# Two more value units in the first eight retention steps, and the first merge set begun four steps later

## The chip, the cores and the metric

One core of a Trainium2 chip runs the whole kernel. The metric is the device time of one execution in microseconds (us); below is better. TensorE (PE in the profile) does the matmuls, its weight loads are listed apart as PEld; VectorE is DVE, ScalarE is ACT, GpSimd is POOL, and SyncE (SP) only issues DMAs and waits for semaphores.

## The reference

One decoder layer on 1,024 tokens of width 1,024, in float32. An input projection of the normed `x` gives ten parts. Two branches are computed from them and merged:

```python
y_mla = mla_branch(...) * silu(gate_mla)            # 8 heads of causal softmax attention, 1024 wide
y_ret = retention_branch(q, k, v, ...) * silu(gate_ret)   # 4 heads, chunks of 128 tokens, v is 2048 wide
merged = sigmoid(merge_mla) * (y_mla @ w_proj_mla) + sigmoid(merge_ret) * (y_ret @ w_proj_ret)
x = x + gate * (merged @ w_out)
```

Retention runs chunk by chunk with a state of 256 x 512 per head: the output of a chunk is `((q k^T) * decay) v + q R`, then `R` is decayed and `k^T v` added, and the output is normalised over 512 values. The value projection `h @ w_in[:, v_ret]` (1024 x 1024 by 1024 x 2048) is a plain matrix product, and so is `y_mla @ w_proj_mla`.

## The kernel before, in words

Every float32 operand is split in two halves (hi on ACT, lo on DVE, each as a rounded type that PE reads), and a product is three matmuls: hi by hi, hi by lo, lo by hi. Every engine's program is one list in a fixed order, written out by hand; an engine waits where it stands.

**The two stages that matter.** Attention is 64 steps (8 heads x 8 query blocks, `STEPS`), named g here with i = g mod 8. In step g PE does the scores of block g (`scores`, L2199 to L2203), half of the step's filler, the values of an earlier pair of blocks in odd steps (L2218 to L2220), the transposes of the probabilities of block g-1 (L2240) and the other half of the filler. `scores(g)` waits until the exponential of block g-1 has been read out of the same PSUM banks (`exp_done`). DVE masks the scores (L1691) and finds their maximum (L1693), ACT takes the exponential (L1283) and then reads its sum out (a second ACT instruction on L1283), DVE normalises. Retention is 32 steps (4 heads x 8 chunks, `CHUNK_STEPS`), named n, with m = n mod 8. In step n PE does the outputs of the chunk (L2289 to L2297; only three matmuls of 512 columns when m = 0), the state (L2307 to L2309; not when m = 7), filler, the key transposes and inner scores of the next chunk, filler, the transposes of the normalised output (`turn_outputs`, L2320) and a last share of filler. DVE's list in step n: the merges of finished set units, statistics of the output (L1794 and on), the low halves of the state (L1810), the masking and halves of the next inner scores (L1770 to L1778), the gated output (L1818), the low halves of the queries and keys two chunks ahead (L1330), and then whatever splits are planned for that step. `turn_outputs` needs ACT's normalised output `out_n` (L1362), and the next outputs need DVE's `inner_lo` (L1778).

**The filler** is matmul work without dependence on the step around it, cut in products of one matmul of 512 columns:

- The *value fill* (`fill`, L2132): 32 units (`FILL_UNITS`), each 24 products (`UNIT`): the value projection for one head and one block of 128 tokens. It is summed in bank `FILL_BANKS[unit % 3]`, evicted by ACT (`evict_fill`, L1319) and DVE (`lower_fill`, L1670) into `v_stage`, and stored by a DMA of GpSimd (`store_fill`, L1055). A unit may begin when the unit three before it, whose bank it takes, is lowered. How many products are done by the end of attention step g stands in `fill_plan`: 42 before the first step, then `FILL_STEP[i]` in every step, `FILL_END` in the three steps behind the last, and `FILL_LATE[n]` in the first retention steps.
- The *first merge set* (`fill_set`, L2164): 16 units of 24 products, `y_mla @ w_proj_mla`, by `set_plan`. Its inputs are loaded and split in the retention steps that `MERGE_LOAD`, `MERGE_SPLIT`, `SET0_LOAD` and `SET0_SPLIT` name.

**Weights of the value fill.** Each group of 8 units (one head of values) has its weights in four parts. Products 12p to 12p+12 of the last pair of units of a group free part p (`parts_used`). In the next step's list SP loads the part of the next group (`load_weight`, L504), ACT splits it behind the copies of the transposed probabilities (`split_weight`, L524, 1,024 columns) and DVE lowers it (`lower_weight`, L530). All these loads but two go through one raw place, so a load waits until the part before it has been lowered. If the last-but-one unit of a group was finished in the step before, its eviction stands ahead of the exponential (`filled_ahead`).

**GpSimd** rotates the queries and keys of chunk n (`rotate_chunk`, L1046 to L1051) as soon as the outputs of chunk n-3 are done. The last two value units are stored ahead of the rotation of chunk 9. The rotated chunk n is rounded by ACT in retention step n-2 (`high_qk`, L1326).

Of the kernel before, what the change touches and what calls it, by code (L numbers as in the profile page):

```python
# [18 lines left out]
ACT = mybir.ActivationFunctionType  # L19
# [5 lines left out]
KD = D // P  # L25
# [60 lines left out]
FILL_UNITS = V_GROUPS * NT  # L86
R_MERGE = len(SEQ)
SETS = 3
MERGE_LOAD = (1, 4, 5, 7)
MERGE_SPLIT = (2, 5, 7, 10)  # L90
SET0_LOAD = {2: (2, 3), 3: (4, 5), 4: (6, 7)}
SET0_SPLIT = {0: (0,), 1: (1,), 3: (2,), 4: (3, 4), 5: (5,), 6: (6, 7)}
# [6 lines left out]
FILL_BANKS = (2, 1, 3)  # L99
# [14 lines left out]
FILL_STEP = [12, 12, 11, 11, 10, 9, 9, 7]  # L114
FILL_END = [12, 10, 8]
FILL_LATE = [12, 12, 12, 12]
UNIT = 3 * KD
CHUNK_STEPS = H_RET * NT


class Layer:
# [267 lines left out]
    def counts(self):  # L389
# [8 lines left out]
        for n in range(CHUNK_STEPS):  # L398
            first, between, last = 12 * max(n - 3, 0), n - 7, 16 * (n - CHUNK_STEPS + 4)
            if last > 0:  # L400
                self.set_plan.append((2 * KD - 2) * UNIT + last)
            elif between > 0:
                self.set_plan.append(2 * UNIT + (2 * KD - 4) * UNIT * between // (CHUNK_STEPS - 11))
            else:
                self.set_plan.append(first)
# [198 lines left out]
    def parts_used(self, step):  # L604

        return sum(2 * UNIT * (4 * g + 3) + 12 * (part + 1) <= self.filled_by(step)
                   for g in range(V_GROUPS - 1) for part in range(V_PARTS))

# [247 lines left out]
    def sync_retention(self, sp):  # L856
        d = self.d
        units = 0
        for n in range(CHUNK_STEPS):
# [6 lines left out]
            if n == 6:  # L866
                self.load_t(sp, 0)
                self.load_t(sp, 1)
# [96 lines left out]
    def gpsimd(self, pool):  # L965
# [59 lines left out]
        for n in range(2, CHUNK_STEPS):  # L1025
            if n == 9:
                for unit in range(units, FILL_UNITS):
                    self.store_fill(pool, unit)
            self.rotate_chunk(pool, n)
# [278 lines left out]
    def evict_fill(self, act, unit):  # L1308
        act.wait_ge(self.fill_summed, unit + 1)
        if unit == 0:  # L1310
            act.wait_ge(self.raw_stored, 16 * RAW)
        elif unit == 1:
            for slot in range(3):
                act.wait_ge(self.split_stored[slot], self.store_count[slot])
        elif unit == 3:
            act.wait_ge(self.v_up_stored[2], 16 * 4)
        if self.v_stores(unit):
            act.wait_ge(self.v_stored[self.v_slot(unit)], 16 * self.v_stores(unit))
        self.nc.scalar.activation(self.v_place(unit)[:, 0, :], self.p[:, FILL_BANKS[unit % 3], :], ACT.Copy,  # L1319
                                  scale=self.t["ret_cols"][:, unit:unit + 1]).then_inc(self.v_hi_ready, 1)  # L1320
# [23 lines left out]
    def scalar_retention(self, act):  # L1344
        nc, p, t = self.nc, self.p, self.t
        units = 0
        for n in range(CHUNK_STEPS):
# [20 lines left out]
            if n == len(FILL_LATE) - 1:  # L1368
                for unit in range(FILL_UNITS - 2, FILL_UNITS):
                    self.evict_fill(act, unit)  # L1370
# [296 lines left out]
    def lower_fill(self, dve, unit):  # L1667
        dve.wait_ge(self.v_hi_ready, unit + 1)
        stage = self.v_place(unit)
        self.nc.vector.scalar_tensor_tensor(out=stage[:, 1, :], in0=self.p[:, FILL_BANKS[unit % 3], :],  # L1670
# [110 lines left out]
    def vector_retention(self, dve):  # L1781
        nc, p, t = self.nc, self.p, self.t
        units = 0
        for n in range(CHUNK_STEPS):
# [37 lines left out]
            if n == len(FILL_LATE) - 1:  # L1822
                for unit in range(FILL_UNITS - 2, FILL_UNITS):
                    self.lower_fill(dve, unit)
# [290 lines left out]
    def fill(self, pe, upto):  # L2115

        while self.filled < upto:
# [6 lines left out]
            if k == 0 and kind == 0:  # L2124
                if unit < 3:
                    pe.wait_ge(self.evicted, self.raws + RAW - 1)
                else:
                    pe.wait_ge(self.v_lo_ready, unit - 2)
# [3 lines left out]
            ins = self.nc.tensor.matmul(self.p[:, FILL_BANKS[unit % 3], :], h[:, k, tok], w[:, cut],  # L2132
# [133 lines left out]
    def inner_scores(self, pe, n):  # L2266
# [3 lines left out]
        if n == 1:  # L2270
            pe.wait_ge(self.v_lo_ready, FILL_UNITS - 2)
# [297 lines left out]
```

## Time and profile before

| | |
|---|---|
| median of 3 runs | 1616.3 us |
| lowest, highest | 1615.83, 1621.77 us |
| profiled execution, span from first to last instruction | 1616.2 us |
| attention, first scores to first retention outputs | 759.9 to 1101.4 us |
| retention, 32 steps | 1101.4 us to about 1347 us |

The only time that the profiled execution left is its span; no other time of its own is recorded, and the span stands 0.1 us under the median of the runs. Of the profile, PE's busy share says little here, since a busy PE can be one whose matmuls are stretched by waits inside the pipeline. What counts is the start of one matmul against the start of the next, the idle time in square brackets behind a row and the engine named there, and the granted clock (PEclk, 1.00 is full speed).

### The profile page before, as it was taken

How to read it: one execution, taken by the hardware profiler on the slowest of the kernel's cores; microseconds unless marked ns; L12 is line 12 of the kernel's file. 1: busy time of each engine (PE TensorE's matmuls, PEld its weight loads, DVE VectorE, ACT ScalarE, POOL GpSimd, SP SyncE). 2: the span in 40 equal slices, each digit the busy share in tenths (PEclk: the TensorE clock that was granted, in tenths of full speed). 3: DMA queues.
4: the chain of work that ended last, by engine and by line, in shares of the span. 5: the costliest groups of instructions: out<-in, count | busy, mean ns of one | idle time of the engine just before them, and what ended most of it. 6: DMA issues, size and time to landing. Idle time of an engine off the chain costs nothing. (4 is left out here: it accounts for less than half of the span.)

```text
span 1616.2 us, 20288 instructions
## 1 busy us (share of the span) xinstructions
PE 1568.4 (97%) x7568; PEld 1308.9 (81%) x7568; DVE 959.4 (59%) x1626; ACT 605.1 (37%) x1057; POOL 322.0 (20%) x280
## 2 busy tenths in 40 slices
PE   5999999999999999999999999899999999999998
PEld 4778888888888888798888888787688888888886
DVE  6984444444444457752566665567987775647544
ACT  5444333333333343342343433334544443213111
POOL 2232223322322200200000000015655530000000
PEclk9999999999999999999999999999999999999999
DMA  9132332223323334799265554447977767345422
GB/s 385 38 130 105 111 112 110 107 109 115 120 104 111 95 97 164 301 414 322 82 209 170 181 184 164 179 137 260 323 235 228 250 204 281 115 137 183 143 105 78
DMA packets 142225, 278.70 MB, mean 172 GB/s; under 512 B 11056, under 2 KB 83632, under 8 KB 133552
## 3 DMA queue, kind: packets, MB, share of 16 engines
q1 hardware_dynamic: 125488, 245.09, 43.6%
q10 hardware_dynamic: 12032, 15.54, 2.9%
q0 software_dynamic: 4608, 16.78, 2.7%
q8 instruction: 61, 1.00, 0.2%
q14 instruction: 36, 0.29, 0.1%
HBM read 182.47 MB, written 94.37 MB: 171 GB/s over the span
## 5 line engine op out<-in xcount | busy, mean ns | idle before, releaser
L1579 DVE TENSOR_TENSOR w_form<-w_pair,w_form 128x512 fp32r<-128x512 f32 x150 | 116.3, 776 | 127.2 <-ACT w_form L1211 125.6
L1211 ACT ACTIVATE w_form<-w_pair 128x512 fp32r<-128x512 f32 x150 | 94.6, 632 | 245.3 <-PE p_banks L2093 237.2
L2090 PE MATMUL p_banks<-h_hi,w_form 128*128 128x512 f32 x300 | 116.8, 389 | 1.1 <-DVE w_form L1579 1.1
L2093 PE MATMUL p_banks<-h_hi,w_form 128*128 128x512 f32 x300 | 116.7, 389 | 0.0
L2092 PE MATMUL p_banks<-h_lo,w_form 128*128 128x512 f32 x300 | 116.7, 389 | 0.0
L1283 ACT ACTIVATE prob<-p_banks,neg_max 128x128 f32<-128x128 f32 (+3 forms) x64 | 47.5, 742 | 182.9 <-DVE neg_max L1693 182.9
L524 ACT ACTIVATE w_hi<-w_raw 128x1024 fp32r<-128x1024 f32 (+2 forms) x69 | 59.5, 866 | 144.9 <-PE p_banks L2348 96.2
L2348 PE MATMUL p_banks<-y_hi,w_lo 128*128 128x512 f32 x256 | 99.6, 389 | 0.0
L2347 PE MATMUL p_banks<-y_lo,w_hi 128*128 128x512 f32 x256 | 99.6, 389 | 0.0
L2346 PE MATMUL p_banks<-y_hi,w_hi 128*128 128x512 f32 x256 | 99.6, 389 | 0.0
L1055 POOL DMA_DIRECT2D v_ret<-v_stage x32 | 17.7, 554 | 410.1 <-DVE v_stage L1670 410.0
L530 DVE TENSOR_TENSOR w_lo<-w_raw,w_hi 128x1024 fp32r<-128x1024 f32 (+3 forms) x70 | 72.0, 1033 | 35.4 <-ACT w_hi L524 34.7
L2132 PE MATMUL p_banks<-w_hi,h_hi 128*128 128x512 f32 x192 | 78.8, 410 | 0.6 <-DVE w_lo L530 0.6
L1008 POOL TENSOR_TENSOR w_pair<-w_pair 128x512 f32<-128x512 f32 x25 | 32.5, 1299 | 232.2 <-DVE w_form L1579 232.2
L2090 PE MATMUL p_banks<-h_sum_hi,w_form 128*128 128x512 f32 x200 | 77.9, 389 | 0.0
L2093 PE MATMUL p_banks<-h_sum_hi,w_form 128*128 128x512 f32 x200 | 77.8, 389 | 0.0
L2092 PE MATMUL p_banks<-h_sum_lo,w_form 128*128 128x512 f32 x200 | 77.8, 389 | 0.0
L2090 PE MATMUL p_banks<-h_forms,w_form 128*128 128x512 f32 x200 | 77.8, 389 | 0.0
L2092 PE MATMUL p_banks<-h_forms,w_form 128*128 128x512 f32 x200 | 77.8, 389 | 0.0
L2093 PE MATMUL p_banks<-h_forms,w_form 128*128 128x512 f32 x200 | 77.8, 389 | 0.0
L2132 PE MATMUL p_banks<-w_lo,h_hi 128*128 128x512 f32 x192 | 76.6, 399 | 0.0
L2132 PE MATMUL p_banks<-w_hi,h_lo 128*128 128x512 f32 x192 | 76.5, 398 | 0.0
(316 smaller groups left out, 4302.7 us busy)
## 6 DMA issues: line engine op xcount, KB each, us to landing
w_pair<-in_w_pairs SPq DMA_DIRECT2D x25, 1024.0 KB, 4.9
w_raw<-in_w_dense SPq DMA_DIRECT2D x45, 512.0 KB, 4.7
v_ret<-v_stage POOLq DMA_DIRECT2D x32, 512.0 KB, 3.4
v_chunk<-v_ret SPq DMA_DIRECT2D x32, 512.0 KB, 3.7
merge_t<-act_t SPq DMA_DIRECT2D x48, 256.0 KB, 3.4
act_t<-stage SPq DMA_DIRECT2D x40, 256.0 KB, 2.0
act_t<-stage_late SPq DMA_DIRECT2D x40, 256.0 KB, 2.0
ada<-in_w_ada SPq DMA_DIRECT2D x4, 2048.0 KB, 23.9
```

What stands on the lines that cost most here:

```text
L524: self.nc.scalar.activation(self.hi_place(r), self.raw_place(r), ACT.Copy).then_inc(self.w_hi_ready, 1)
L530: self.nc.vector.tensor_tensor(self.lo_place(r), self.raw_place(r), self.hi_place(r).bitcast(F32), ALU.subtract)\
L1211: self.nc.scalar.activation(self.form[f % FORM_SLOTS][:, 0, :], self.form_source(f), ACT.Copy).then_inc(self.form_hi, 1)
L1283: nc.scalar.activation(self.prob[:, g % 2, 0:width], p[:, 6:8, :].rearrange("p a n -> p (a n)")[:, 0:width], ACT.Exp, bias=self.neg_max[:, ...
L1579: nc.vector.tensor_tensor(self.form[f % FORM_SLOTS][:, 1, :], self.form_source(f), self.form[f % FORM_SLOTS][:, 0, :].bitcast(F32), ALU.su ...
L2090: self.nc.tensor.matmul(out, w_hi[:, cut], x_hi[:, q, :], start=fresh and q == 0, stop=False, skip_group_check=True)
L2092: self.nc.tensor.matmul(out, w_hi[:, cut], x_lo[:, q, :], start=False, stop=False, skip_group_check=True)
L2093: last = self.nc.tensor.matmul(out, w_lo[:, cut], x_hi[:, q, :], start=False, stop=q == KD // 2 - 1, skip_group_check=True)
L2132: ins = self.nc.tensor.matmul(self.p[:, FILL_BANKS[unit % 3], :], h[:, k, tok], w[:, cut], start=(k == 0 and kind == 0), stop=(k == KD - 1 ...
L2346: self.nc.tensor.matmul(out, self.w_hi[:, slot, cut], self.y_hi[y][:, tok], start=(k == 0), stop=False)
L2347: self.nc.tensor.matmul(out, self.w_hi[:, slot, cut], self.y_lo[y][:, tok], start=False, stop=False)
L2348: return self.nc.tensor.matmul(out, self.w_lo[:, slot, cut], self.y_hi[y][:, tok], start=False, stop=(k == KD - 1))
```

## The change

The steps of attention lose 6 filler products per head (`FILL_STEP` from a sum of 81 to one of 75), 48 in all, and `FILL_LATE` holds 12 products for eight retention steps in place of four. So 28 of the 32 units are done at the first retention step, not 30. Units 28 to 31 take banks 1 and 2 by turns, since bank 3 holds the inner scores. They are evicted in retention steps 1, 3 and 7 and stored ahead of the rotations of chunks 4, 6 and 11. Loads and splits of the first merge set move to later steps, the set begins in step 8, and its 288 middle products are spread over 17 steps and not 21.

```diff
-MERGE_LOAD = (1, 4, 5, 7)
-MERGE_SPLIT = (2, 5, 7, 10)
-SET0_LOAD = {2: (2, 3), 3: (4, 5), 4: (6, 7)}
-SET0_SPLIT = {0: (0,), 1: (1,), 3: (2,), 4: (3, 4), 5: (5,), 6: (6, 7)}
+MERGE_LOAD = (5, 8, 9, 11)
+MERGE_SPLIT = (6, 9, 11, 14)
+SET0_LOAD = {6: (2, 3), 7: (4, 5), 8: (6, 7)}
+SET0_SPLIT = {0: (0,), 2: (1,), 7: (2,), 8: (3, 4), 9: (5,), 10: (6, 7)}
...
-FILL_STEP = [12, 12, 11, 11, 10, 9, 9, 7]
+FILL_STEP = [11, 11, 10, 10, 9, 9, 8, 7]
 FILL_END = [12, 10, 8]
-FILL_LATE = [12, 12, 12, 12]
+FILL_LATE = [12] * 8
+LATE_UNIT = {1: (28,), 3: (29,), 7: (30, 31)}
+LATE_STORE = {4: (28,), 6: (29,), 11: (30, 31)}
+LATE_UNITS = 4
...
-            first, between, last = 12 * max(n - 3, 0), n - 7, 16 * (n - CHUNK_STEPS + 4)
+            first, between, last = 12 * max(n - 7, 0), n - 11, 16 * (n - CHUNK_STEPS + 4)
...
-                self.set_plan.append(2 * UNIT + (2 * KD - 4) * UNIT * between // (CHUNK_STEPS - 11))
+                self.set_plan.append(2 * UNIT + (2 * KD - 4) * UNIT * between // (CHUNK_STEPS - 15))
...
+    def fill_bank(self, unit):
+
+        return FILL_BANKS[unit % 3] if unit < FILL_UNITS - LATE_UNITS else 1 + unit % 2
...
-            if n == 6:
+            if n == 10:
                 self.load_t(sp, 0)
                 self.load_t(sp, 1)
...
-            if n == 9:
-                for unit in range(units, FILL_UNITS):
-                    self.store_fill(pool, unit)
+            for unit in LATE_STORE.get(n, ()):
+                self.store_fill(pool, unit)
             self.rotate_chunk(pool, n)
...
-            if n == len(FILL_LATE) - 1:
-                for unit in range(FILL_UNITS - 2, FILL_UNITS):
-                    self.evict_fill(act, unit)
+            for unit in LATE_UNIT.get(n, ()):
+                self.evict_fill(act, unit)
...
-            if n == len(FILL_LATE) - 1:
-                for unit in range(FILL_UNITS - 2, FILL_UNITS):
-                    self.lower_fill(dve, unit)
+            for unit in LATE_UNIT.get(n, ()):
+                self.lower_fill(dve, unit)
...
-                    pe.wait_ge(self.v_lo_ready, unit - 2)
+                    pe.wait_ge(self.v_lo_ready, unit - (2 if unit <= FILL_UNITS - LATE_UNITS else 1))
...
-            pe.wait_ge(self.v_lo_ready, FILL_UNITS - 2)
+            pe.wait_ge(self.v_lo_ready, FILL_UNITS - LATE_UNITS)
```

## Rows read from the trace of the kernel before

**Rows 1.** The page's head: the span, and PE's busy time, share and instructions.

```profile
span 1616.2 us, 20288 instructions
PE 1568.4 (97%) x7568; PEld 1308.9 (81%) x7568; DVE 959.4 (59%) x1626; ACT 605.1 (37%) x1057; POOL 322.0 (20%) x280
```

**Rows 2.** Busy time by stretch: the stretch, its length, each engine (instructions), PEclk, DMA, GB/s.

```profile
200.00:300.00 100.00, 100.00 (x443) 82.79 (x442) 45.65 (x65) 36.69 (x64) 27.62 (x20) 1.00 0.30 111
759.90:1101.40 341.50, 333.79 (x1902) 288.98 (x1901) 209.62 (x448) 123.02 (x269) 24.87 (x37) 0.99 0.50 168
1133.50:1173.80 40.30, 36.59 (x177) 27.53 (x176) 36.54 (x86) 23.25 (x44) 23.19 (x24) 1.00 0.98 324
```

**Rows 3.** Who waited for whom, PE: us in total, times, the longest.

```profile
PE p_banks L2199 <- ACT prob L1283: 7.5, 3, 3.5
PE p_banks L2320 <- ACT out_n L1362: 5.6, 9, 1.1
```

**Rows 4.** Instructions in order of time, PE at the end of step 35 (start, duration, idle before).

```profile
935.80 0.39 PE L2132 MATMUL p_banks<-w_hi,h_hi 128*128 128x512 f32 x1
938.43 0.50 PE L2199 MATMUL p_banks<-k_even,q_even 128*128 128x512 f32 x1 [2.24 <-ACT prob L1283]
```

**Rows 5.** In order of time: end of the sum's read-out, next scores (ends of steps i = 4, 6).

```profile
899.60 0.20 ACT L1283 ACTIVATION_READ_ACCUMULATOR prob<-p_banks,neg_max 128x1 f32 x1
900.01 0.40 PE L2199 MATMUL p_banks<-k_odd,q_odd 128*128 128x512 f32 x1
...
870.08 0.19 ACT L1283 ACTIVATION_READ_ACCUMULATOR prob<-p_banks,neg_max 128x1 f32 x1
870.32 0.50 PE L2199 MATMUL p_banks<-k_even,q_even 128*128 128x512 f32 x1
```

**Rows 6.** In order of time: two weight parts in adjacent steps, and the scores behind them.

```profile
1009.84 1.05 ACT L524 ACTIVATE w_hi_aside<-w_raw 128x1024 fp32r<-128x1024 f32 x1
1012.18 0.33 SPq L504 DMA_DIRECT2D w_raw<-in_w_dense  x1
1016.92 1.06 ACT L524 ACTIVATE w_hi<-w_raw 128x1024 fp32r<-128x1024 f32 x1 [2.98 <-DMA w_raw<-in_w_dense]
1020.79 0.19 ACT L1283 ACTIVATION_READ_ACCUMULATOR prob<-p_banks,neg_max 128x1 f32 x1
1021.03 0.50 PE L2199 MATMUL p_banks<-k_even,q_even 128*128 128x512 f32 x1 [1.75 <-ACT prob L1283]
```

**Rows 7.** Landing of the weight loads in attention; one slow load; PEclk behind it.

```profile
DMA to landing us min/median/max: 3.6/3.8/12.0
...
1027.92 0.35 SPq L504 DMA_DIRECT2D w_raw<-in_w_dense  x1
...
1035.26 1.06 ACT L524 ACTIVATE w_hi<-w_raw 128x1024 fp32r<-128x1024 f32 x1 [3.87 <-DMA w_raw<-in_w_dense]
...
1040.00:1050.00 10.00, 9.90 (x44) 8.47 (x45) 4.87 (x10) 3.00 (x7) 0.00 (x0) 0.69 0.04 13
```

**Rows 8.** In order of time, retention step 4: splits at its head, statistics, the transposes, next outputs.

```profile
1135.31 1.40 DVE L1670 SCALAR_TENSOR_TENSOR v_stage<-p_banks,ret_cols,v_stage 128x512 fp32r<-128x512 f32 x2
...
1137.76 0.69 DVE L1794 BATCH_NORM_STATS2 stats<-p_banks 128x6 f32<-128x512 f32 x1
...
1140.78 0.66 PE L2320 MATMUL p_banks<-ident,out_n 128*128 128x128 f32 x4 [1.07 <-ACT out_n L1362]
...
1142.41 0.50 PE L2289 MATMUL p_banks<-v_chunk,inner_hi 128*128 128x512 f32 x1
```

**Rows 9.** In order of time, DVE: the same split beside a rotation on GpSimd, and without.

```profile
1110.39 2.31 DVE L1839 TENSOR_TENSOR y_lo<-y_raw,y_hi 128x1024 fp32r<-128x1024 f32 x1
...
1118.72 1.21 DVE L1839 TENSOR_TENSOR y_lo<-y_raw,y_hi 128x1024 fp32r<-128x1024 f32 x1
```

**Rows 10.** In order of time: the rotation of chunk 4 begins; ACT rounds the rotated chunk.

```profile
1114.12 1.28 POOL L1046 TENSOR_TENSOR qk_by_sine_early<-qk_raw 128x512 f32<-128x512 f32 x1
...
1125.63 0.62 ACT L1326 ACTIVATE qk_chunk<-qk_raw 128x512 fp32r<-128x512 f32 x1
```

More of the change, by code:

```diff
@@ L1318, in evict_fill @@
             act.wait_ge(self.v_stored[self.v_slot(unit)], 16 * self.v_stores(unit))
-        self.nc.scalar.activation(self.v_place(unit)[:, 0, :], self.p[:, FILL_BANKS[unit % 3], :], ACT.Copy,
+        self.nc.scalar.activation(self.v_place(unit)[:, 0, :], self.p[:, self.fill_bank(unit), :], ACT.Copy,
                                   scale=self.t["ret_cols"][:, unit:unit + 1]).then_inc(self.v_hi_ready, 1)
@@ L1669, in lower_fill @@
         stage = self.v_place(unit)
-        self.nc.vector.scalar_tensor_tensor(out=stage[:, 1, :], in0=self.p[:, FILL_BANKS[unit % 3], :],
+        self.nc.vector.scalar_tensor_tensor(out=stage[:, 1, :], in0=self.p[:, self.fill_bank(unit), :],
                                             scalar=self.t["ret_cols"][:, unit:unit + 1], in1=stage[:, 0, :].bitcast(F32),
@@ L2131, in fill @@
             w = self.lo_place(r) if kind == 2 else self.hi_place(r)
-            ins = self.nc.tensor.matmul(self.p[:, FILL_BANKS[unit % 3], :], h[:, k, tok], w[:, cut],
+            ins = self.nc.tensor.matmul(self.p[:, self.fill_bank(unit), :], h[:, k, tok], w[:, cut],
                                         start=(k == 0 and kind == 0), stop=(k == KD - 1 and kind == 2))
```

## The prediction

> **What bounds the kernel now.** I read the page's head first: PE is busy for 97% of the span [rows 1], so what can be won is PE's own stalls. The list of who waited for whom names the two places where this change acts: scores that wait for an exponential, 7.5 us in 3 waits, and the output transposes of retention that wait for the normalised output, 5.6 us in 9 [rows 3]. The view by stretch adds what these lists hide: retention steps 4 to 8 have a PE busy 36.59 of 40.30 us beside a DVE busy 36.54 [rows 2]; that stretch is bound by DVE, the rest of retention by PE.
>
> A filler product costs what a matmul of 512 columns costs at full speed, 100 us / 443 = 0.226 us [rows 2]. The same work stays on PE wherever the plan puts it. **So the 48 moved products are worth nothing by themselves**: attention loses 48 x 0.226 = 10.8 us, retention gains 10.8. Only stalls decide, in four places.
>
> **1. Steps in which attention already waits.** The shortest time from the read-out of an exponential's sum to the next scores is 0.05 us: 1020.79 + 0.19 to 1021.03, a real wait [rows 6]. At the end of an i = 6 step it is 870.08 + 0.19 to 870.32, also 0.05 [rows 5]. There PE arrives no later than the exponential, so the product taken from that step (9 to 8) leaves a hole: 8 heads x 0.23 = **+1.8**. At the end of i = 4 the slack is 900.01 - 899.80 = 0.21, 0.16 above the least [rows 5]; a product less leaves 0.06, **+0.5** over 8 heads. The other steps that lose one had about 1 us or more. Bounds: 0 if those steps' other waits move along, +3.6 if every product taken from i = 4 and 6 is lost whole.
>
> **2. The weight parts.** Before, parts are freed in steps 10, 11, 13, 14; 29, 31, 32, 33; 48, 49, 51, 52 (the fill plan crossing 156, 168, 180, 192 and so on, 192 products to a group). Rows 6 show what two adjacent steps cost. A split at 1009.84 must be lowered before the next load goes out at 1012.18, the load's data come 4.7 us later, and ACT, which has the next exponential behind that split, sits idle for 2.98 us; PE then idles 1.75. The three such waits are the 7.5 us of [rows 3]: 2.24 [rows 4], 1.75 [rows 6] and 3.5, the last behind a load that took 7.3 us, 1027.92 to 1035.26 [rows 7], because query and key loads had gone out in front of it. After that wait PEclk is 0.69 over 10 us [rows 7]: 6.2 us at 1.2 instead of 2.4 GHz, 3.1 us lost. Together **10.6 us**.
>
> By the new plan parts are freed in 11, 12, 14, 15; **32, 33, 34, 35**; 52, 53, 55, 56. From one split to the next at least 2.3 (ACT and DVE) + 3.6 to 4.7 (landing, [rows 6, 7]) = 5.9 to 7.0 us pass, while an attention step lasts 341.5 us / 67 = 5.1 [rows 2], and steps 34 to 36 about 4. The middle group needs three intervals in a row: 18 to 21 us against some 13.5 of steps; with the slacks there (1, 1.4 us) I get 2.6 us idle ahead of scores(36). A second effect: the last two units of a group now end in the same step (6 and 7 in 15, 14 and 15 in 35, 22 and 23 in 56), so the unit after next asks for a bank that DVE has only just got to. DVE lowers unit 14 behind the part, the mask, the maximum and the gated output, some 2.5 us after the part; PE stands at its third product after the transposes. That makes 3.4 us in step 36, and by the same working 1.8 in step 16 and 2.0 in step 57. The first group adds 1.0 in step 14, where the slack is nil. Sum 1.0 + 1.8 + 2.6 + 3.4 + 2.0 = 10.8, so **+0.2**. The third group's long wait goes, the second's takes its place. Bounds: 4 (landings of 3.6, units lowered in time) and 18 (a landing of 7.3, and the half clock behind the second group).
>
> **3. The DVE-bound steps of retention.** In step 4, DVE's backlog (two unit lowerings, 1.40, and a 1.21 split) puts the statistics off to 1137.76; the transposes follow 3.02 later with 1.07 idle, and the next outputs 4.65 after the statistics [rows 8]. After the change steps 4 to 6 carry none of these splits, and their stalls (about 1.6 + 0.8 + 0.8) go. But the same splits stand in steps 7 to 11, and step 8 is the first of a head: six output matmuls fewer, 1.4 us, hide less. It stays 8.9 us long, 3.0 of them stall; steps 9 to 11 give 0.8 each, step 12 (two merges and a weight) 0.5, step 7 0.3. Before, this stretch is 3.7 us idle by [rows 2], and 6.4 by the starts of its matmuls in steps 4 to 12 (stretched matmuls hide the rest); after, 0.3 + 3.0 + 2.4 + 0.5 = 6.2: **-0.2**. Bounds: 3 and 9.
>
> **4. Denser filler behind.** From step 12 on 17 products a step stand in place of 14, two of the three ahead of the transposes, 0.45 us. Steps 15 and 23, where no state is computed, waited 0.67 and 0.19 idle, some 0.8 and 0.3 in the starts; 1.0 of that goes. Stalls of steps 0 to 3 are the same, but the stored unit 28 now goes ahead of the rotation of chunk 4 on GpSimd. That rotation began at 1114.12 and is used at 1125.63 [rows 10]; behind the lowering of unit 28 (about 1119.5) and a store of 0.55 it ends near 1124.2, still in time. But the next one then runs beside DVE's split. A split took 2.31 us beside a rotation and 1.21 alone [rows 9]; of that 1.1 I take 0.3, with 0 and 1.1 as ends. Places 3 and 4: -0.2 - 1.0 + 0.3 = **-0.9**.
>
> The Trainium skill, "SBUF — State Buffer", under "Who interferes with whom", holds that the port pair of DVE and GpSimd is an exclusive lock: one waits for the other's whole instruction. By that each of the three displaced rotations could cost a split its full 1.3 us, and the sum would be up to 4 us more. Rows 9 fit it in size, but the rotation slowed too, and most DVE work there reads PSUM.
>
> Loads of the set on SP move with their steps, past nothing that waits longer: they are 512 KB each and needed one step later, as before. The bank waits of units 28 to 31 are for units lowered a step or more ahead. I cost these at nothing; if that cover went, it would be a part of a step, 1 us.
>
> **The sum**: 1616.2 + 2.3 + 0.2 - 0.9 = 1617.8. It is made against the span, 0.1 us under the median, so the forecast is 1617.8 us: **no change that can be measured**. Against no change this kernel can be told apart to about 0.5%, 8 us.
>
> **Rivals.** *The clusters dissolve* (faster). The third group spreads over 52, 53, 55, 56 and its 3.5 us wait and half clock go; if the second group pays only what two adjacent steps pay, 2.2 us, and the bank waits are hidden, place 2 falls from 10.6 to 3: 1610. If in addition retention's steps 8 to 11 keep up, 1607. For it: the first group before had adjacent parts (10, 11 and 13, 14) and no PE wait at all. Against: four adjacent steps, and the 5.9 us floor. Chance 0.25.
>
> *The middle group breaks the pace* (slower). Four parts in 32 to 35, PE idle for over 2 us twice within 12 us. If PEclk falls behind it as at 1040 [rows 7], 3.1 us come on top, and if one landing takes 7.3 in place of 3.8, 3.5 more: 1617.8 + 6.6 = 1624.4. It decides from the point where the idle time ahead of scores(37) passes the 3.5 us that went before the drop at 1040. For: the same pair of waits preceded that drop. Against: 2.24 us at 936 [rows 4] brought none. Chance 0.2.
>
> The Trainium skill, "TensorE: Matmul & The Clock Gate", in "Part 1: The HAM clock gate", says that an idle array goes back to 1.2 GHz and returns to 2.4 after sustained work. Rows 7 agree; where it says the drop comes would favour this rival.
>
> *Retention swallows the products* (slightly faster): stalls of steps 8 to 12 shrink to 3, since set products could fill them: 1614. Chance 0.15. *The forecast's own case*: 0.4.
>
> **How the numbers follow.** Forecast's own range 1614 to 1621. For 8 in 10 I reach down to 1608 and up to 1624. Faster by over 0.5% (under 1608.2): a third of the first rival and a little of the third, 0.11. Slower by over 0.5% (over 1624.4): under half of the second, 0.09. The rest, 0.80, is within.
>
> **What would show it.** After: scores that wait for exponentials in the second group, at steps 36 and 37, and none of 3.5 us in the third; value products (L2132) waiting for DVE's `v_stage` at steps 16, 36, 57; idle of 0.2 us ahead of scores at every i = 7; retention steps 4 to 6 near 7.1 us long, step 8 near 8.9. It is wrong if steps 32 to 37 show no waits, or if the lists of waits together fall by over 8 us.

## The result and the profile after

The changed kernel takes 1621.1 us (median of 12 runs, 1620.2 to 1624.8), the kernel before, in turn on the same chip, 1617.3 (12 runs, 1615.0 to 1621.8). The ratio is 1.0023 (95% interval 1.0013 to 1.0033): 3.7 us or 0.23% slower, within the 0.5% that the forecast called no change. The interval leaves 1 out, so this is a small loss that can be measured, not no change. Forecast were 1617.8 us and +1.6; 1621.1 lies 0.1 us above the forecast's own range (1614 to 1621) and inside the wider one (1608 to 1624). The profiled execution spans 1620.6 us, 4.4 more than before; the terms below are read from it.

The page's head, the view by stretch (columns as in [rows 2]; line numbers of the kernel after are 3 to 6 higher, so that its L2203 is L2199 of before) and the waits of PE:

```profile
span 1620.6 us, 20288 instructions
PE 1569.7 (97%) x7568; PEld 1307.9 (81%) x7568; DVE 964.3 (60%) x1626; ACT 606.3 (37%) x1057; POOL 327.3 (20%) x280
```

```profile
758.70:1094.60 335.90, 325.56 (x1854) 279.85 (x1854) 208.76 (x446) 122.42 (x267) 23.47 (x35) 0.99 0.49 169
1126.90:1167.50 40.60, 37.84 (x188) 30.38 (x187) 33.71 (x81) 20.04 (x39) 26.38 (x27) 1.00 0.90 308
...
940.00:945.00 5.00, 2.52 (x6) 2.04 (x7) 4.57 (x11) 3.01 (x5) 1.07 (x2) 0.67 0.79 283
945.00:950.00 5.00, 5.00 (x24) 4.37 (x23) 2.46 (x5) 0.99 (x2) 0.00 (x0) 0.65 0.96 333
```

```profile
PE p_banks L2136 <- DVE v_stage L1675: 5.8, 3, 3.2
PE p_banks L2324 <- ACT out_n L1368: 5.0, 7, 1.7
...
PE p_banks L2203 <- ACT prob L1289: 3.3, 2, 2.6
```

Attention takes 335.8 us in place of 341.5, with 48 products fewer (x1854 against x1902 in [rows 2]). Those products alone are 10.8 us; only 5.7 went. From retention's first outputs to the end it is 526.0 against 514.9, +11.2, nearly the 10.8 that were moved there. The rest is -1.1 before the first scores, where the change does nothing: that point lies anywhere from 758.8 to 761.4 us in the fourteen traces of this study, and no edit touches what stands ahead of it. A difference of 1 or 2 us between two single traces is therefore to be read from the steps that an edit touches, not from the spans. Of the waits, scores behind exponentials fell from 7.5 to 3.3 us [rows 3], and a form that had stood at 0.2 us before took their place: value products that wait for VectorE to lower a unit, 5.8 us.

Both meet in steps 35 and 36. In order of time:

```profile
931.55 1.06 ACT L527 ACTIVATE w_hi<-w_raw 128x1024 fp32r<-128x1024 f32 x1 [3.37 <-DMA w_raw<-in_w_dense]
...
932.70 0.39 PE L2136 MATMUL p_banks<-w_lo,h_hi 128*128 128x512 f32 x1
...
933.90 0.33 SPq L507 DMA_DIRECT2D w_raw<-in_w_dense  x1
...
935.67 0.50 PE L2203 MATMUL p_banks<-k_even,q_even 128*128 128x512 f32 x1 [2.59 <-ACT prob L1289]
...
936.01 0.39 PE L2204 MATMUL p_banks<-k_even,q_even 128*128 128x512 f32 x1
936.24 0.39 PE L2205 MATMUL p_banks<-k_even,q_even 128*128 128x512 f32 x1
...
937.73 1.06 ACT L527 ACTIVATE w_hi<-w_raw 128x1024 fp32r<-128x1024 f32 x1 [1.73 <-DMA w_raw<-in_w_dense]
...
938.82 1.23 DVE L533 TENSOR_TENSOR w_lo<-w_raw,w_hi 128x1024 fp32r<-128x1024 f32 x1 [2.02 <-ACT w_hi L527]
938.88 0.40 PE L2136 MATMUL p_banks<-w_lo_aside,h_hi 128*128 128x512 f32 x1
...
941.68 0.74 DVE L1675 SCALAR_TENSOR_TENSOR v_stage<-p_banks,ret_cols,v_stage 128x512 fp32r<-128x512 f32 x1
...
942.48 0.79 PE L2136 MATMUL p_banks<-w_hi_aside,h_hi 128*128 128x512 f32 x1 [3.20 <-DVE v_stage L1675]
943.07 0.63 PE L2136 MATMUL p_banks<-w_hi_aside,h_lo 128*128 128x512 f32 x1
943.50 0.63 PE L2136 MATMUL p_banks<-w_lo_aside,h_hi 128*128 128x512 f32 x1
```

The reader is to see three things. ScalarE had idled 3.37 us for the load of the split at 931.55, the exponential stood behind that split, and PE idled 2.59 us ahead of its scores. At 938.82 VectorE lowers the next part, then does the mask, maximum and gated output, and reaches the unit at 941.68; PE stands 3.20 us for it. Behind that second stop the products follow each other every 0.43 us where they took 0.23 (936.01 to 936.24): the granted clock is 0.67 and 0.65 in the view above, 1.2 GHz for part of each stretch. That costs 2.4 us more.

### The profile page after: what moved, and what is told of

The parts are those of the page before. It is cut to its first block and busy times, and to the rows that moved or that the text cites. A ratio compares the mean times of both kernels' runs of the same rounds, so it can differ in the third digit from the quotient of the medians.

```text
span 1620.6 us, 20288 instructions
## 1 busy us (share of the span) xinstructions
PE 1569.7 (97%) x7568; PEld 1307.9 (81%) x7568; DVE 964.3 (60%) x1626; ACT 606.3 (37%) x1057; POOL 327.3 (20%) x280
## 5 line engine op out<-in xcount | busy, mean ns | idle before, releaser
L533 DVE TENSOR_TENSOR w_lo<-w_raw,w_hi 128x1024 fp32r<-128x1024 f32 (+3 forms) x70 | 72.5, 1040 | 31.4 <-ACT w_hi L527 30.8
```

What stands on the lines that cost most here:

```text
L533: self.nc.vector.tensor_tensor(self.lo_place(r), self.raw_place(r), self.hi_place(r).bitcast(F32), ALU.subtract)\
```

## The experiments

"Lost" means, here and below, the distance from the start of a matmul to the next start, less the median distance for its kind; a step runs from its first scores (in retention, its first output matmul) to the next step's. Every ratio is to the kernel before, run in turn with it; each interval is about 0.001 to either side, and each kernel left one trace.

**One product back into i = 6.**

```
-FILL_STEP = [11, 11, 10, 10, 9, 9, 8, 7]
+FILL_STEP = [11, 11, 10, 10, 9, 9, 9, 6]
```

> One value product a head goes back from the step with i = 7 (7 to 6) into the step with i = 6 (8 to 9), the group's parts stay in the same steps. Theory (place 1 of the prediction: PE arrives at the scores of i = 7 before the exponential of i = 6, so a product put there is free): the gap of 0.52 us ahead of those scores falls to about 0.29 in all 8 heads, 8 x 0.23 = 1.8 us less than the changed kernel's 1621.1, so 1619.3. Rival (the product is missed at the end of i = 7 instead, where the next scores then wait): no change, 1621. The clusters at steps 35 to 37 and their half clock stay either way (PE idle of 2.6 and 3.2 us, granted clock near 0.65 from 942 to 949).

Measured: 1620.2 us, 1.0019 (1.0010 to 1.0028). The interval overlaps that of the changed kernel, so the 1 us is not shown by the times. In the trace the distance ahead of the scores of i = 7 is 0.28 in place of 0.52 us in the heads without parts, and such a head lasts 39.07 in place of 39.38 us: the hole is real and closes. But 1.8 us are lost at steps 17 and 19, by value products that wait. The middle group still idles 3.0 us in one piece, at the end of which the clock falls for a shorter time (1.0 us lost). Place 1 holds; its gain is partly taken by a wait that had been covered. The edit did more than its expectation says: it also ends unit 6 a step sooner (step 14 in place of 15), and the 1.2 us that PE idled for a unit in step 16 is gone in this trace.

**The unit lowered ahead of the mask.**

```
+            if self.filled_ahead(g) and units < self.units_filled(g - 1):
+                self.lower_fill(dve, units)
+                units += 1
             if g < STEPS:
                 cell = slice(g % 4, g % 4 + 1)
...
-            if self.filled_ahead(g) and units < self.units_filled(g - 1):
-                self.lower_fill(dve, units)
-                units += 1
```

> VectorE lowers the next-to-last unit of a group ahead of its step's mask and maximum, in place of behind them and behind the gated output; nothing else moves. Theory (the bank wait is one of order on VectorE, and the second idle of the middle group is what drops the clock): the idle ahead of the value products in steps 16, 36 and 57 (1.5, 3.4, 1.5 us in the changed kernel) falls to 0, 1.5 and 0, the clock stays up behind step 36 (3 us), and 0.7 us of later exponential comes back in each of the three steps: 1621.1 - 4.9 - 3 + 2.1 = 1615.3. Rival 1 (the landing of the weight parts sets both idles; the order only shifts them): the scores of the same steps wait as much longer, 1621, with the half clock. Rival 2 (the clock falls behind the 2.6 us ahead of step 36's scores alone): 1618.3, with the granted clock still near 0.65 behind step 36.

Measured: 1620.7 us, 1.0034 (1.0021 to 1.0047). Rival 1 in the times; the waits for a unit fall, as in the theory, and the scores wait more, as in rival 1:

```profile
PE p_banks L2203 <- ACT prob L1289: 4.6, 3, 2.5
PE p_banks L2136 <- DVE v_stage L1675: 2.1, 2, 1.4
```

Three stops of 2.6, 1.6 and 1.5 us lost stand in steps 35 and 36, and yet the clock stays up:

```profile
935.00:940.00 5.00, 3.61 (x18) 2.73 (x18) 2.18 (x5) 2.80 (x5) 0.00 (x0) 1.00 0.45 134
940.00:945.00 5.00, 2.35 (x10) 1.66 (x11) 4.27 (x10) 2.33 (x5) 0.53 (x1) 1.00 0.68 221
```

So in this run the idle of 2.5 us ahead of step 36's scores brought no half clock, and rival 2 does not hold here; a run below shows that the same idle can bring it. Attention is 3.2 us shorter in this trace (332.7), retention 2.2 longer, with a stretch of half clock in its step 2 (1.6 us) that the changed kernel's trace does not have. With five runs, and this trace from one of the slower ones, the gain in attention is not shown by the times.

**Parts split a step later, behind the exponential.**

```
 (ScalarE, behind the exponential; VectorE the same behind the normalising)
+            while parts < self.parts_used(g - 2):
+                self.split_weight(act, R_V + V_PARTS + parts)
+                parts += 1
...
-            while parts < self.parts_used(g - 1):
```

> ScalarE splits a freed weight part, and VectorE lowers it, one step later and behind that step's exponential and normalising, in place of ahead of the next exponential. The loads are issued at the same points. Theory (an exponential is held by a split that waits for its DMA): the idle ahead of the scores of steps 15 and 36 (0.9 and 2.6 us) goes, the bank waits shrink where they came behind a held exponential (3.4 to about 1.5 in step 36), and with them the half clock of 3 us: 1621.1 - 0.6 - 2.6 - 1.9 - 3 = 1613. Rival (the split is then late for the copies of the transposed probabilities behind it, and PE waits for these instead, some 1.2 us in each of 12 steps of which half is covered): 1621.1 - 5 + 7 = 1623.

Measured: 1618.6 us, 1.0014 (1.0006 to 1.0023), span 1616.2. No scores wait for an exponential in the list of waits any more; the unit's waits are down to

```profile
PE p_banks L2136 <- DVE v_stage L1675: 3.2, 2, 2.3
```

and in the stretch that held the half clock the granted clock is full:

```profile
934.00:944.00 10.00, 6.69 (x42) 5.39 (x41) 7.54 (x14) 4.01 (x8) 1.07 (x2) 1.00 0.61 193
```

Attention is 5.4 us shorter than the changed kernel's, less than the theory has, since stops of 0.6, 1.1 and 1.3 us at value products (steps 17, 37, 59) came up. The spans differ by 4.4 us, as retention is 0.9 longer with a drop of the clock in its step 10, and the medians by 2.5, about half-way between theory and rival; what lies between the two figures one trace can't tell. Steps 35 to 37 take 18.0 us in place of 23.3 and steps 14 to 17 take 22.6 in place of 23.7. That shows for these two groups that an exponential held by a split that waits for its load was the first link. The third group, where no scores waited, is 1.3 us longer.

**Another order of the same 75 products.**

```
+FILL_STEP = [8, 10, 10, 9, 11, 10, 11, 6]
```

> The same 75 products a head, laid over its eight steps as 8, 10, 10, 9, 11, 10, 11, 6: parts come free in steps 12, 13, 14, 15; 32, 33, 35, 36; 52, 54, 55, 57, the last two units of each group end in different steps, and the steps with i = 4 and 6 have 1 and 3 products more. Theory (the cost of the change in attention is a matter of which steps the plan picks, not of the 48 moved products): holes of place 1 go (2.3 us), the bank waits go (1.5 + 3.4 + 1.5), the idle ahead of step 36 falls from 2.6 to about 1, no half clock (3): 1621.1 - 12 = 1609, with 3 us either way. Rival (parts in four steps in a row, 12 to 15, or three products fewer at i = 0, cost as much as is won): the first group takes over the wait of the middle one with its half clock, 1618 to 1621.

Measured: 1627.8 us, 1.0072 (1.0058 to 1.0085): the worst kernel of all, 6.7 us over the changed one, where I expected 12 under. The holes of place 1 did go (0.23 us ahead of the scores of i = 5 and 7 in all heads but one, a head without parts 38.8 us). But the middle group still idled, 2.8 us ahead of step 36's scores, and behind it the clock fell to 1.2 GHz for the whole stretch; and in step 59 the value products waited 3.6 us for their head's values:

```profile
935.00:940.00 5.00, 4.71 (x13) 3.84 (x14) 2.68 (x7) 1.32 (x5) 0.00 (x0) 0.50 1.02 388
```

```profile
1047.06 0.53 ACTq L771 DMA_DIRECT2D v_head<-v_hl  x1
...
1057.60 0.58 PE L2222 MATMUL p_banks<-pt_hi,v_head 128*128 128x256 f32 x1 [3.55 <-DMA v_head<-v_hl]
```

That load is issued just ahead of the scores of a head's step i = 2, when the last head's values are free, and is used in the middle of step i = 3. It lands in 5.9 to 7.3 us in the changed kernel (median 6.0) and here in up to 10.5, beside a weight part, stores of value units and chunk loads. The holes at the ends of other steps may have been part of its slack; this trace does not separate them from the late landing. The trace's span is only 3.4 us over the changed kernel's, since the profiled execution was the fastest of the five; the rest of the 6.7 us stays unexplained.

**Retention: the second tile's split behind step 4.**

```
-SET0_SPLIT = {0: (0,), 2: (1,), 7: (2,), 8: (3, 4), 9: (5,), 10: (6, 7)}
+SET0_SPLIT = {0: (0,), 4: (1,), 7: (2,), 8: (3, 4), 9: (5,), 10: (6, 7)}
```

> The split of the set's second tile moves from the end of retention step 2 to the end of step 4; nothing else moves. Theory (the term of 0.3 us for GpSimd beside VectorE was too small: the step behind that split is held by a lowering that took 2.32 us beside a rotation): step 3 falls from 8.37 to about 7.35 us, step 5 stays near 7.3 since no unit is lowered there, so 1.0 us less than the changed kernel: 1620.1. Rival 1 (the split only carries its own 1.2 us and the contention to step 5): 0, 1621.1, step 5 at 8.3. Rival 2 (the transfers or the rotation itself hold step 3): step 3 stays at 8.37.

Measured: 1623.2 us, 1.0048 (1.0033 to 1.0063), 2 us over even rival 1. Its mechanism is there: step 3 falls from 8.37 to 7.30 us and step 5 grows from 7.32 to 8.79. The split meets a rotation there as well; the only one up to 1150 took

```profile
L1843 DVE TENSOR_TENSOR y_lo<-y_raw,y_hi x1: 2307/2307/2307, 1137.3 to 1137.3; 128x1024 fp32r<-128x1024 f32 x1
```

against 2.32 in the changed kernel's step 3. Step 10 lost 0.9 more as well, with a drop of the clock at its end.

**Retention: chunk loads first.**

```
             if n + 3 < CHUNK_STEPS:
                 self.load_v_chunk(sp, n + 3)
+            if n + 4 < CHUNK_STEPS:
+                self.load_qk_chunk(sp, n + 4)
             if n in MERGE_LOAD:
...
-            if n + 4 < CHUNK_STEPS:
-                self.load_qk_chunk(sp, n + 4)
```

> In retention the loads of query and key chunks and of their table go out ahead of the merge weights' and the set's, in place of behind them; these then go out about 3 us later. Theory (the rotations of steps 8 to 11 start late because their chunk lands behind 512 KB loads, and so run beside VectorE's splits; steps 8 and 10 pay 1 to 1.7 us each for it): rotations start 1 to 2 us sooner, step 10 falls from 9.58 to about 8.2 and step 8 from 9.24 to about 8.5: 1621.1 - 2 = 1619. Rival 1 (contention only meets another instruction of VectorE): steps 8 to 11 together stay within 0.5 us of 35.1. Rival 2 (the splits now wait for the set's loads, which land a step later): 1621.1 + 3, waits of ScalarE on the set's loads.

Measured: 1619.6 us, 1.0021 (1.0011 to 1.0031). The theory in the steps: step 8 takes 8.61 in place of 9.24 us and step 10 takes 8.05 in place of 9.58; steps 4 to 12 lose 7.7 in place of 9.9 us. The times don't tell it from the changed kernel. In the changed kernel the rotation ahead of step 10's end began only at 1170.07, after 5.89 us of idle for its table, and ran into three of VectorE's instructions, which it stretched and which stretched it:

```profile
1170.07 1.29 POOL L1052 TENSOR_TENSOR qk_by_sine<-qk_raw 128x512 f32<-128x512 f32 x1 [5.89 <-DMA qk_raw<-ret_tables]
...
1172.11 1.19 DVE L1336 TENSOR_TENSOR qk_chunk<-qk_raw,qk_chunk 128x512 fp32r<-128x512 f32 x1
1172.83 1.07 POOL L1056 TENSOR_TENSOR qk_raw<-qk_raw,qk_by_sine 128x256 f32<-128x256 f32 x1
1173.22 1.76 DVE L533 TENSOR_TENSOR w_lo<-w_raw,w_hi 128x1024 fp32r<-128x1024 f32 x1
1173.85 1.72 POOL L1057 TENSOR_TENSOR qk_raw<-qk_raw,qk_by_sine 128x256 f32<-128x256 f32 x1
1174.90 1.76 DVE L1843 TENSOR_TENSOR y_lo<-y_raw,y_hi 128x1024 fp32r<-128x1024 f32 x1
1175.71 2.09 POOL L1052 TENSOR_TENSOR qk_by_sine<-qk_raw 128x512 f32<-128x512 f32 x1
1176.58 0.69 DVE L1799 BATCH_NORM_STATS2 stats<-p_banks 128x6 f32<-128x512 f32 x1
```

With the loads first, that rotation starts after 3.97 us of idle and its last part takes 0.73 us in place of 1.72:

```profile
1165.73 1.40 POOL L1052 TENSOR_TENSOR qk_by_sine<-qk_raw 128x512 f32<-128x512 f32 x1 [3.97 <-DMA qk_raw<-ret_tables]
...
1169.27 0.73 POOL L1057 TENSOR_TENSOR qk_raw<-qk_raw,qk_by_sine 128x256 f32<-128x256 f32 x1
...
1171.01 0.68 DVE L1336 TENSOR_TENSOR qk_chunk<-qk_raw,qk_chunk 128x512 fp32r<-128x512 f32 x1
1171.67 1.23 DVE L533 TENSOR_TENSOR w_lo<-w_raw,w_hi 128x1024 fp32r<-128x1024 f32 x1
1172.81 1.22 DVE L1843 TENSOR_TENSOR y_lo<-y_raw,y_hi 128x1024 fp32r<-128x1024 f32 x1
```

VectorE's three instructions, now clear of the rotation, take 1.58 us less together, and the step is 1.53 us shorter: the stretching is what the late rotation cost.

Nothing in attention was edited here, and its scores of step 36 come after the same idle of 2.59 us as in the changed kernel. There the clock stayed up behind it; here it fell:

```profile
937.20 0.64 PE L2203 MATMUL p_banks<-k_even,q_even 128*128 128x512 f32 x1 [2.59 <-ACT prob L1289]
```

```profile
935.00:940.00 5.00, 2.81 (x9) 2.33 (x10) 2.41 (x6) 1.84 (x4) 0.00 (x0) 0.74 0.47 134
```

**The late splits in the kernel before.** The edit of the late splits, on the other kernel.

> The kernel BEFORE the change, with the weight parts split and lowered one step later, behind that step's exponential. Theory (the 10.6 us that its weight parts cost, 7.5 idle and 3.1 of half clock, come from exponentials held by splits): the waits of 2.2, 1.75 and 3.5 us ahead of scores go, and the half clock behind 1040 with them; 3 us come back as bank waits and waits of value products as in the changed kernel with the same edit: 1617.0 - 7.6 = 1609.4. Rival (only the distance between the four landings counts, wherever the splits stand: the same time is lost at the copies of transposed probabilities): 1615 to 1617.

Measured: 1615.2 us, 0.9998 (0.9988 to 1.0007): the rival in the times. The three waits and the half clock behind 1040 are gone (steps 35, 51 and 54 take 4.78, 4.62 and 4.85 in place of 7.02, 6.53 and 8.45 us), but the third group still loses 3.7 us at other points (stops of 1.3 us for a unit in step 52 and 1.8 for lowered probabilities in step 55), and the first group, which had cost nothing, now stops PE: an exponential's successor, the copy of transposed probabilities, stands behind the split.

```profile
842.78 1.06 ACT L524 ACTIVATE w_hi<-w_raw 128x1024 fp32r<-128x1024 f32 x1 [1.06 <-DMA w_raw<-in_w_dense]
843.87 1.23 DVE L530 TENSOR_TENSOR w_lo<-w_raw,w_hi 128x1024 fp32r<-128x1024 f32 x1 [1.64 <-ACT w_hi L524]
846.35 0.19 PEld L2218 LDWEIGHTS p_banks<-pt_hi,v_head 128*128 128x128 f32 x1 [2.30 <-DVE pt_lo L1727]
```

**Three edits together on the changed kernel.** The late splits, FILL_STEP = [11, 11, 10, 9, 10, 9, 9, 6], and the second tile's split behind step 4.

> The changed kernel with the late splits, the products laid as 11, 11, 10, 9, 10, 9, 9, 6 (one more at i = 4 and at i = 6, so no hole there, and units 14 and 15 end in steps 35 and 36), and the second tile's split behind step 4. Theory (the terms are independent): against the late splits alone (1618.6) the holes give 2.3 us back, the bank wait of step 36 another 2.5, retention step 3 another 1.0: 1612.8. Rival (the holes are slack for the load of the next head's values, which takes 6 us from issue to landing; where a weight part lands beside it, value products wait for it instead): 1616 to 1618, with idle of 1 us and more ahead of value products at steps 17, 19, 37 and 59.

Measured: 1618.9 us, 1.0013 (1.0003 to 1.0023): the rival, and 0.9 us over its range. Attention is as long as with the late splits alone (330.1 against 330.4 us): a head without parts is shorter, and 2.4 us are lost at step 59 and 1.0 at step 17 by value products, 2.2 of it waiting for the head's values. The terms were not independent.

**Parts on a schedule of their own.** On the kernel before:

```
+PART_DUE = (11, 12, 14, 15, 30, 32, 34, 36, 49, 52, 54, 55)
...
+    def parts_due(self, step):
+
+        return sum(due <= step for due in PART_DUE)
...
 (the same in the lists of SyncE, ScalarE and VectorE)
-            while parts < self.parts_used(g - 1):
+            while parts < self.parts_due(g):
```

> The kernel BEFORE the change, with the twelve weight parts of attention split, lowered and reloaded by a list of steps of its own (ends of steps 11, 12, 14, 15; 30, 32, 34, 36; 49, 52, 54, 55) in place of as soon as they are free (11, 12, 14, 15; 30, 32, 33, 34; 49, 50, 52, 53). No product moves. Theory (what the parts cost is set by the distance from one split to the next against about 6 us of lowering, issue and landing, and by the slack of the exponential behind the split): the waits of 2.2, 1.75 and 3.5 us and the half clock of 3.1 go, 0 to 2 us come back elsewhere: 1616.7 - 9.5 = 1607. Rival (as with the late splits on this kernel, the waits turn up at value products, which lack lowered probabilities or the next head's values): 1614 to 1616.

Measured: 1617.1 us, 1.0003 (0.9991 to 1.0014), over the theory and the rival alike. The scores no longer wait, and PE waits as long for the parts themselves, which its products reach before they are lowered:

```profile
PE p_banks L2137 <- DVE w_lo L531: 7.1, 3, 3.3
```

A miss of mine: I had each group begin some six products later than it does. On the changed kernel, with the one product moved and the chunk loads first, the same mistake:

> The changed kernel with three edits: parts at the ends of steps 12, 14, 15, 16; 33, 36, 38, 39; 53, 54, 56, 57; the products as 11, 11, 10, 10, 9, 9, 9, 6; chunk loads of retention ahead of the set's. Theory (each acts alone): 1621.1 - 0.9 (step 15) - 2.6 (step 36) - 1.9 of the bank wait of 3.4 - 2.4 (half clock) - 1.8 (holes) - 1.5 (chunk loads, measured) = 1610. Rival 1 (holes filled are value loads waited for: 1.8 us at steps 17 and 19, as when the product moved alone): 1612. Rival 2 (a bank wait is one of the unit's lowering, whatever the parts do, and stays at 3.4 with its half clock): 1615.

> The kernel of the changed parts' steps, products and chunk loads, and VectorE lowering a group's next-to-last unit ahead of its mask and maximum. Theory (with the parts out of the way an earlier lowering is worth the bank wait): 1.5, 1.5 and 1.5 us of bank waits go at steps 16, 36 and 57, 0.7 each comes back through the later exponential only where the slack is nil: 2 to 3 us under the kernel without this edit. Rival (the later exponential gives all of it back, as it did in the changed kernel alone, 1620.7 to 1621.1): the same within 1 us.

Measured: 1619.0 us, 1.0010 (1.0001 to 1.0019), over the theory and both rivals, and 1618.5 us, 1.0014 (1.0005 to 1.0023). The scores of the middle group no longer wait; 4.8 us go to the parts:

```profile
PE p_banks L2141 <- DVE w_lo L534: 4.8, 2, 3.6
```

PE idles only 0.7 us for the unit in step 36, where it had been 3.2: that wait came mostly from the parts in front of it on VectorE. Steps 8 and 10 of retention are 8.16 and 8.05 us in the first of the two; with the chunk loads first alone they were 8.61 and 8.05. The lowered unit ahead of the mask again wins nothing that the times show. The three show that a part has two deadlines, the exponential that its split may hold and the product that uses it, and that only one of them had been in my model.

**The kernel before, eight of its twelve parts late.**

```
 (ScalarE, behind the exponential; VectorE the same behind the normalising)
+            while V_PARTS <= parts < self.parts_used(g - 2):
+                self.split_weight(act, R_V + V_PARTS + parts)
+                parts += 1
...
-            while parts < self.parts_used(g - 1):
+            while parts < min(V_PARTS, self.parts_used(g - 1)):
```

> The kernel BEFORE the change with its first four weight parts split as before (no wait of PE belonged to them) and the other eight one step later, behind that step's exponential. Theory (where a split stands is right or wrong step by step: late splits took 2.2 to 3.7 us waits and a half clock away in the second and third group, and put 0.7, 0.4 and 2.0 us into the first, where there was nothing to win): against all parts late (profile 1613.2, median 1615.2) 3.1 us less, so 1612, and steps 14 to 17 again 4.85, 6.88, 4.01 and 6.40 us. Rival (the time that goes in one place comes back in start-up, at the entry of retention or as a drop of the clock elsewhere, as the eleven runs so far have it): 1614 to 1617, no difference from before that can be told.

Measured: 1611.9 us (12 runs, 1609.5 to 1618.0) against 1616.4, 0.9974 (0.9963 to 0.9985): the theory, and 4.5 us under the kernel before (2.4 to 6.0 by the interval, whose upper end touches the rival's 1614). It beats both kernels. Its span is 1607.7 us; attention and the stretch that had held the 3.5 us stop:

```profile
760.20:1094.10 333.90, 331.11 (x1901) 286.80 (x1900) 209.69 (x448) 122.77 (x269) 24.92 (x37) 1.00 0.51 172
1035.00:1045.00 10.00, 9.29 (x59) 7.95 (x57) 7.48 (x16) 4.59 (x10) 0.00 (x0) 1.00 0.28 110
```

Attention takes 333.9 us in place of 341.5 with all of its products, less than the changed kernel needs with 48 fewer. Steps 14 to 17 are 4.85, 6.87, 4.01 and 6.40 us as expected. The trace flatters it: the profiled execution was the fastest of the twelve, and 1.6 of its 8.5 us under the trace of before are a stretch of half clock in retention step 2 that did not come, where nothing was edited. What is left to win is in steps 52 and 55, which lose 1.6 and 1.0 us.

## Why the prediction was right, and where it was off

The main statement held: the moved products are worth nothing by themselves (attention -10.8 of products, the rest +11.2), and what is left is the account of the stalls. That account was 2.8 us short by the traces (4.4 measured, 1.6 forecast), and about 4 short if the 1.1 us ahead of attention, which the change does not touch, are left out. All three of its terms were too small, each by 1.3 or 1.4 us, and the last would have been off by 2.9 but for a stretch of half clock that did not come this time (1.6 us, below). That the total came as near as it did is in part luck. The statement that 8 us is the least that can be told apart was too coarse as well: the interval is 1.6 us to either side. By its places:

- **Place 1, forecast +2.3, measured 3.7.** A head without parts takes 39.38 us against 40.27, -0.89 where six products are 6 x 0.226 = 1.36: 0.47 a head, 8 x 0.47 = 3.7 (0.19 at the end of i = 4, 0.21 at the end of i = 6, the rest small). The hole ahead of i = 7 is as forecast:

```profile
908.10 0.19 ACT L1289 ACTIVATION_READ_ACCUMULATOR prob<-p_banks,neg_max 128x1 f32 x1
...
908.35 0.19 PEld L2203 LDWEIGHTS p_banks<-k_odd,q_odd 128*128 128x128 f32 x1 [0.56 <-ACT prob L1289]
```

  0.52 us from product to scores against 0.29. At i = 4 the step that failed is "a product less leaves 0.06": the idle is 0.07, but a chain of matmuls that has stopped also takes 0.10 us longer from its first matmul to its second (0.34 from 935.67 to 936.01, 0.23 after that), and this stop is new in every head; by the step lengths i = 4 and the step behind it lose 0.19 us a head where 0.06 was forecast.
- **Place 2, forecast 10.8 against 10.6, measured 12.9 against 11.3, +1.6.** Scores of step 36: forecast 2.6, idle 2.59. Unit waits of steps 16, 36, 57: forecast 1.8, 3.4, 2.0, lost 1.5, 3.4, 1.5. Step 14: forecast 1.0, 0.9. The forecast had scores of step 37 waiting in "what would show it"; they did not (a distance of 0.43 us), the stop was the unit's alone. Third group: its 3.5 us wait gone, as forecast. The term that I left at zero is the half clock behind the middle group, 2.4 us lost: this part of the slower rival came true, at a price of 2.4 where it said 3.1, without its slow landing (3.8 from 933.90 to 937.73) and without the condition that it was tied to, over 3.5 us idle ahead of the scores of step 37: PE had stood 2.59 and 3.20 us at other points. And 0.5 us at step 11, where values landed late, was in no term.
- **Places 3 and 4, forecast -0.9, measured +0.4.** Steps 4 to 6 are 7.32 us (forecast near 7.1), step 8 is 9.24 (8.9), steps 9 and 11 lose 0.9 and 0.8 (0.8 each), step 7 0.4 (0.3). Step 10 lost 2.3 where 0.8 stood. Steps 4 to 12 together lose about 1.5 us more than in the trace of before when both are counted by the same rule; the prediction had 6.2 against 6.4. Step 3 lost 1.0 to a split beside a rotation:

```profile
1118.87 2.32 DVE L1843 TENSOR_TENSOR y_lo<-y_raw,y_hi 128x1024 fp32r<-128x1024 f32 x1
1120.18 1.60 POOL L1056 TENSOR_TENSOR qk_raw<-qk_raw,qk_by_sine_early 128x256 f32<-128x256 f32 x1
...
1125.76 0.50 PE L2293 MATMUL p_banks<-v_chunk,inner_hi 128*128 128x512 f32 x1 [0.83 <-DVE inner_lo L1783]
```

  So the term that failed is "of that 1.1 I take 0.3": it was 1.0 in step 3 and some 1.5 in step 10, and the chunk loads alone brought the latter back. I had said that the set's loads move "past nothing that waits longer"; true of the issue on SP, but the chunk loads behind them land later, and GpSimd waits for those. Against that, step 2 is 1.6 us shorter than before (7.33 against 8.92), since a stretch of half clock there did not come; no term had it. It is there in six of the fourteen traces, among them two kernels that differ from the changed one only in attention. Steps 15 and 23 gave 0.7 in place of 1.0.

Sum: 3.7 + 1.6 + 0.4 - 1.1 (ahead of attention) = 4.6, against 4.4 of the two spans.

The Trainium skill, "SBUF — State Buffer", under "Who interferes with whom", says that a VectorE instruction with two inputs in SBUF contends with a GpSimd instruction that reads SBUF. The rows of step 10 agree on who is hit: the lowered weight and tile (two inputs in SBUF) take 1.76 for 1.21, while the statistics from PSUM, beside a rotation too, keep their 0.69. Its lock for a whole instruction, which the prediction priced at up to 4 us, is not what those rows show in full: both sides stretch, GpSimd's 0.73 to 1.72 and its 1.28 to 2.09. The total, about 2.5 us in steps 3 and 10, lies between my 0.3 and its 4, nearer to its side.

Not settled: which of the clock's drops comes when. In the six traces whose longest stop in the middle group was 2.5 us or less the clock stayed up there, and in the eight with 2.6 us or more it fell; but a stop of 2.24 us in step 59 had a drop behind it. Why step 2 of retention has one in some traces and not in others is open too. Nor was a kernel tried in which the weight parts are smaller or have a second place to land, which might shorten the 6 us between two splits.

## What to carry to other kernels

When filler work moves, price first what it covered: a product taken from a step that already waits leaves a hole, and one put into such a step is free only until the next thing with no slack, here a 6 us load, comes to the fore. A transfer's consumer on an in-order engine has two deadlines, one for what stands behind it on its engine and one for who uses the data; in the kernel before, moving all such consumers one step later won nothing that the times show, and moving only those of the two groups in which some held an exponential won 4.5 us. A plan chosen with the parts, the units and the holes in mind but not the load of the values was the worst kernel of the study, so read a new plan's waits before believing its sum.

## What the runs showed of the hardware

- **The same stop brings the half clock in one run and not in the next.** An idle of 2.59 us ahead of step 36's scores left the clock at 1.00 in the changed kernel and took it down (0.74 over 5 us) in the kernel that differs from it only later, in retention. Of 2.24 us, one left it up (before, at 936 to 938) and one, ahead of value products of step 59 with the three edits together, took it down (0.72 over 1055 to 1060). Stops of 2.5, 1.4 and 1.3 us close together left it up. Of 2.8 us, two took it down (2.77, the other order of products: 0.50; 2.82, the parts' own schedule in the kernel before: 0.68 behind it) and one did not (2.85, the tile's split behind step 4: 1.00 and 0.97). The eight stops of 3.0 to 3.6 us in attention all had a drop that began in them or right behind. Retention has drops behind shorter ones: in its step 2, behind stops of 1 to 2 us, in six traces of fourteen (8.9 us in place of 7.3 or 7.4). A stop of PE thus carries a chance of some 1 to 3 us beyond its idle time that no single trace prices. The Trainium skill, "TensorE: Matmul & The Clock Gate", in "Part 1: The HAM clock gate", makes recent activity the condition of the full clock; that each drop looked at here began in or behind a stop agrees, and which stops get one no row here tells.
- **A stop costs more than its idle**: between the first two matmuls of 512 columns behind it 0.34 us in place of 0.23 at full clock (935.67 to 936.01), and 0.59 in place of 0.43 at half clock (942.48 to 943.07).
- **A load of 6 us took 10.5** when other loads and stores were under way beside it, and PE then waited 3.6 us where the plan left it no slack.
- **VectorE and GpSimd stretch each other.** A lowering of 1,024 columns took 1.76 to 2.32 us beside a rotation and 1.22 or 1.23 clear of it, and the rotation's part of 0.73 took 1.60 and 1.72 at the same time.
